# First norm by feature in four units behind raw turned rows

## The reference, cut to what matters

```python
sc, scc = silu(c), silu(c_ctx)                    # one latent, one context condition
for layer in range(2):
    mod_lat = split(sc @ ada_w[layer] + ada_b[layer], 6)     # each (1024,)
    mod_ctx = split(scc @ ada_w[layer] + ada_b[layer], 6)
    h_lat = rms_norm(x, pre_mix_g[layer]) * (1 + mod_lat[1]) + mod_lat[0]
    h_ctx = rms_norm(ctx, pre_mix_g[layer]) * (1 + mod_ctx[1]) + mod_ctx[0]
    p_lat, p_ctx = h_lat @ w_in[layer], h_ctx @ w_in[layer]
    ...   # two attentions per layer, output projection, sandwich norm
    ...   # second modulated norm, convolution feed-forward, norm
```

## Time and profile before

| what | value |
|---|---|
| median of 3 runs | 1719.2 us (1719.05 to 1720.28) |
| the profiled execution | 1719.3 us |
| its span, first to last instruction | 1717.6 us |
| TensorE busy | 1657.2 us, 96% of the span |
| VectorE, ScalarE, GpSimd busy | 1006.1, 637.0, 233.4 us |
| DMA | 211.36 MB, mean 123 GB/s |
| mean granted TensorE clock | 0.992 of full speed |

### The profile page before, as it was taken

The page is one execution under the profiler, slowest core; times in us unless marked ns, Lnnn a source line. Parts: engine busy times, 40 slices in busy tenths (PEclk is TensorE's granted clock), DMA queues, the critical chain, the costliest instruction groups (busy, mean ns, idle before and its releaser), DMA issues.

```text
span 1717.6 us, 26527 instructions
## 1 busy us (share of the span) xinstructions
PE 1657.2 (96%) x9828; PEld 1334.1 (78%) x9828; DVE 1006.1 (59%) x1912; ACT 637.0 (37%) x1123; POOL 233.4 (14%) x378
## 2 busy tenths in 40 slices
PE   6999899999999999999999999998999999999998
PEld 2877566668898888888878878886678888888886
DVE  4655566754747777777776496315753744443445
ACT  3414555653421212121324443225543533333343
POOL 0413233330100000000000023204420100000000
PEclk9999999999999999999999999998999999999999
DMA  8687231266513353434334454323404443332243
GB/s 318 191 275 220 81 91 35 45 89 213 179 50 99 98 147 98 140 105 130 114 101 146 140 183 140 121 88 55 123 16 135 124 122 98 96 95 66 86 135 135
DMA packets 242584, 211.36 MB, mean 123 GB/s; under 512 B 54201, under 2 KB 204601, under 8 KB 242489
## 3 DMA queue, kind: packets, MB, share of 16 engines
q1 hardware_dynamic: 236186, 199.28, 39.0%
q0 software_dynamic: 4288, 9.10, 1.4%
q10 hardware_dynamic: 2016, 1.73, 0.4%
HBM read 186.58 MB, written 23.48 MB: 122 GB/s over the span
## 4 chain that ended last, share of the span: by engine, by line
PE 86%; DVE 5%; ACT 4%; DMA 2%; issue 2%; SPq 1%; POOL 1%; ACTq 0%; DVEq 0%
PE ps L1361 31%; PE ps L889 10%; PE ps L891 10%; PE ps L890 10%; PE ps L1126 4%; PE ps L1237 4%; PE ps L1032 3%; PE ps L1184 3%; PE ps L1371 2%; PE ps L1175 1%; PE ps L1347 1%; PE ps L1346 1%; PE ps L1345 1%; ACT arena L1727 1%; PE ps L946 1%
## 5 line engine op out<-in xcount | busy, mean ns | idle before, releaser
L1903 DVE TENSOR_TENSOR w_lo<-w_raw,w_hi 128x2048 fp32r<-128x2048 f32 (+3 forms) x112 | 204.0, 1822 | 244.0 <-ACT w_hi L1510 243.3
L889 PE MATMUL ps<-w_hi,act_hi 128*128 128x512 f32 (+2 forms) x872 | 337.6, 387 | 2.6 <-DVE act_lo L1903 1.4
L890 PE MATMUL ps<-w_lo,act_hi 128*128 128x512 f32 (+2 forms) x872 | 333.0, 382 | 0.0
L891 PE MATMUL ps<-w_hi,act_lo 128*128 128x512 f32 (+2 forms) x872 | 332.9, 382 | 0.0
L1361 PE MATMUL ps<-act_lo,w_hi 128*128 128x512 f32 (+1 forms) x912 | 277.8, 359 | 0.0
L1361 PE MATMUL ps<-act_hi,w_hi 128*128 128x512 f32 (+1 forms) x912 | 276.2, 357 | 0.0
L1361 PE MATMUL ps<-act_hi,w_lo 128*128 128x512 f32 (+1 forms) x912 | 274.3, 355 | 0.0
L1510 ACT ACTIVATE w_hi<-w_raw 128x2048 fp32r<-128x2048 f32 (+2 forms) x106 | 166.1, 1567 | 270.0 <-PE ps L891 211.9
L889 PEld LDWEIGHTS ps<-w_hi,act_hi 128*128 128x128 f32 x872 | 164.2, 188 | 39.5 <-issue 9.3
L891 PEld LDWEIGHTS ps<-w_hi,act_lo 128*128 128x128 f32 x872 | 164.2, 188 | 30.8
L890 PEld LDWEIGHTS ps<-w_lo,act_hi 128*128 128x128 f32 x872 | 164.4, 189 | 29.3
(11 more groups left out here) (157 smaller groups left out, 2098.4 us busy)
## 6 DMA issues: line engine op xcount, KB each, us to landing
arena<-in_ada_w SPq DMA_DIRECT2D x44, 1024.0 KB, 8.2
w_raw<-in_ffn_up SPq DMA_DIRECT2D x88, 512.0 KB, 5.2
w_raw<-in_ffn_down SPq DMA_DIRECT2D x88, 256.0 KB, 3.0
w_raw<-in_odd_w_in SPq DMA_DIRECT2D x20, 512.0 KB, 4.5
arena<-mods SPq DMA_DIRECT2D x16, 512.0 KB, 7.0
x_after_mix<-arena SPq DMA_DIRECT2D x10, 512.0 KB, 3.0
arena<-x_after_mix SPq DMA_DIRECT2D x10, 512.0 KB, 6.3
wide_raw<-in_ada_w SPq DMA_DIRECT2D x4, 1024.0 KB, 13.8
```

Of the source, the lines that this page charges most:

```text
L889: mm(out_, s_hi, m_hi, start=start, stop=False)
L890: mm(out_, s_hi, m_lo, start=False, stop=False)
L891: return mm(out_, s_lo, m_hi, start=False, stop=stop)
L1903: V.tensor_sub(out_, full, hi.bitcast(fp32)).then_inc(sem_, 1)
```

## The change

The six row tiles are loaded first, each into its own buffer. They are squared, scaled in place by their root alone and turned raw; ScalarE copies the turned rows to `x_turned`. Shift and scale are now applied by feature, as a value per partition. The four modulation units are cut otherwise: unit n holds the 256 columns of shift and the 256 of scale that belong to feature chunks 2n and 2n + 1 (runs of 1 KB instead of 2 KB). `wide_mm(n)` is followed by a copy of its row to SBUF and by `wide_turn(n)`, four small matmuls with a selector that turn the row into columns; VectorE adds the bias and forms (1 + scale) x gain. Then, for each stream, ScalarE writes the high half of chunks 2n and 2n + 1 from the turned rows (two instructions), VectorE computes the full value (two) and subtracts (one), and `products` multiplies these two chunks for all tiles of the stream. `wide_mm(n + 1)` stands ahead of unit n's products. `ada_mm(0)` and `ada_mm(1)` move to the last unit. Identity and selector are asked for right behind the conditions; the first weight unit is asked for behind the rows, the second behind wide unit 2. Five constants are asked for behind unit 1's high halves, five behind unit 2's, one behind unit 3's. Early modulation units 0 and 1 and weight units 2 and 3 now wait for `wide_mm(1)`, early unit 2 for the last low half of the norm. On POOL the root has two instructions instead of one, since the mean and epsilon move there.

```diff
-        wide_row = arena[:, 8 * D:10 * D]
-        wide_raw = [arena[:, 14 * D + n * KC * WIDE:14 * D + (n + 1) * KC * WIDE].rearrange("p (k c) -> p k c", k=KC)
-                    for n in range(2)]
-        wide_raw += [nc.alloc_sbuf_tensor_at(f"wide_raw{n}", [P, KC, WIDE], fp32, offset=act_at + n * 4 * KC * ROWS)
-                     for n in range(2)]
-        sel = sb("sel", [P, 2, P])
+        x_turned = arena[:, 0:KC * ROWS].rearrange("p (k r) -> p k r", k=KC)
+        x_first = [kilo(6 + t) for t in range(NT)]
+        wide_row = arena[:, 22 * D:22 * D + WIDE]
+        wide_raw = [arena[:, n * D:(n + 4) * D].rearrange("p (k c) -> p k c", k=KC) for n in (14, 18, 10, 14)]
+        first_full = nc.alloc_sbuf_tensor_at("first_full", [P, KC, ROWS], fp32, offset=act_at + 4 * KC * ROWS)
+        first_scrap = nc.alloc_sbuf_tensor_at("first_scrap", [P, 2, D], fp32, offset=act_at + 4 * (KC * ROWS + 5 * ROWS))
+        sel = sb("sel", [P, 2])
...
-        ADA_AT = {(1, 5): [0, 1], (2, 1): [2], (2, 3): [3], (2, 5): [4], (3, 1): [5], (3, 3): [6], (3, 5): [7],
+        ADA_AT = {(1, 0): [0], (1, 1): [1], (2, 1): [2], (2, 3): [3], (2, 5): [4], (3, 1): [5], (3, 3): [6], (3, 5): [7],
...
             def wide_unit(n):
-                v = I["ada_w"][0].rearrange("(k p) c -> p k c", p=P)[:, :, n * WIDE:(n + 1) * WIDE]
+                v = I["ada_w"][0].rearrange("(k p) c -> p k c", p=P)
                 for half, (a, b) in enumerate(((0, KC // 2), (KC // 2, KC))):
-                    sp.dma_start(wide_raw[n][:, a:b, :], v[:, a:b, :]).then_inc(wide_in[n][half], 16)
+                    for part in range(2):
+                        src = v[:, a:b, part * D + n * FEATS:part * D + (n + 1) * FEATS]
+                        sp.dma_start(wide_raw[n][:, a:b, part * FEATS:(part + 1) * FEATS], src)\
+                            .then_inc(wide_in[n][half], 16)
+            def first_rows(t):
+                sp.dma_start(x_first[t], x_source("norm0", t)).then_inc(first_in[t], 16)
+            for t in range(NT):
+                first_rows(t)
+            k_unit(0, I["even_w_in"][0], 0, 4, 0, MLA_IN)
             wide_unit(0)
-            sp.wait_ge(wide_clear, 1)
-            sp.dma_start(wide_row[0:2, :], I["ada_b"][0:1, 0:2 * D].to_broadcast([2, 2 * D])).then_inc(wide_bias, 16)
-            for n in range(1, WIDES - 1):
-                wide_unit(n)
-            gain_loads("norm0")
-            wide_unit(WIDES - 1)
-            x_moves("norm0", range(2))
-            for n in range(2):
-                k_unit(n, I["even_w_in"][0], 4 * n, 4, 0, MLA_IN)
-            x_moves("norm0", range(2, NT))
+            wide_unit(1)
+            sp.wait_ge(t_done, 2 * NT)
+            wide_unit(2)
+            k_unit(1, I["even_w_in"][0], 4, 4, 0, MLA_IN)
+            sp.wait_ge(t_done, row_round(0) + 1)
+            wide_unit(3)
...
-            sp.wait_ge(t_free, WIDES)
+            sp.wait_ge(t_done, row_round(1) + 1)
             for i in range(2):
                 early_unit(i)
             for n in (2, 3):
                 k_unit(n, *units[n])
-            sp.wait_ge(h_ready, base("norm0", "h") + NT)
+            sp.wait_ge(first_lo, 2 * WIDES)
...
             def wide_mm(n):
-                ring_free(n)
+                r = row_round(n)
+                ring_free(r)
...
+            def wide_turn(n):
+                r = row_round(n) + 1
+                pe.wait_ge(t_free, r)
+                for c in range(WIDE // P):
+                    last = mm(bank(6 + r % 2, 2, 2 * c), wide_row[:, c * P:(c + 1) * P], sel[:, :], start=True, stop=True)
+                last.then_inc(t_done, 1)
...
-            def first_norm_turns():
+            def first_norm_products():
+                def rows_turn(t):
+                    pe.wait_ge(h_ready, t + 1)
+                    for half in range(2):
+                        r = turn_round(t) + half
+                        turn(r, r, [x_first[t][:, (4 * half + k) * P:(4 * half + k + 1) * P] for k in range(4)])
+                def products(n, tiles, part):
+                    weights(n // 2)
+                    pe.wait_ge(first_lo, part)
+                    for t in tiles:
+                        rows = slice(t * P, (t + 1) * P)
+                        for j in range(FEAT_K):
+                            k, at = n * FEAT_K + j, (n % 2 * FEAT_K + j) * MLA_IN
+                            cols = slice(at, at + MLA_IN)
+                            last = three(bank(t, MLA_IN), act_hi[:, k, rows], act_lo[:, k, rows],
+                                         w_hi[:, n // 2, cols], w_lo[:, n // 2, cols], k == 0, k == KC - 1)
+                        if n % 2:
+                            last.then_inc(mm_done, 1)
+                latent, context = range(LT), range(LT, NT)
                 for t in range(NT):
...
+                    rows_turn(t)
+                wide_mm(0)
+                wide_turn(0)
+                wide_mm(1)
+                products(0, latent, 1)
+                wide_turn(1)
+                products(0, context, 2)
+                wide_mm(2)
+                products(1, latent, 3)
+                wide_turn(2)
+                products(1, context, 4)
+                wide_mm(3)
+                products(2, latent, 5)
+                wide_turn(3)
+                products(2, context, 6)
+                ada_mm(0)
+                products(3, latent, 7)
+                ada_mm(1)
+                products(3, context, 8)
...
+            for dst, src in FIRST:
+                act.dma_start(dst, src, allow_slow_non_contiguous=True).then_inc(ident_in, 16)
...
-            for dst, src in FIRST:
-                act.dma_start(dst, src, allow_slow_non_contiguous=True).then_inc(ident_in, 16)
...
+            def first_norm():
+                def square(t):
+                    act.wait_ge(first_in[t], 16)
+                    at_least(act, sum_x, t - 1)
+                    A(first_scrap[:, t % 2, :], x_first[t], ACT.Square, accum_out=ssx[:, t:t + 1]).then_inc(sum_x, 1)
+                def turned(t):
+                    for half in range(2):
+                        r = turn_round(t) + half
+                        act.wait_ge(t_done, r + 1)
+                        A(x_turned[:, 4 * half:4 * half + 4, t * P:(t + 1) * P],
+                          bank(6 + r % 2).rearrange("p (k r) -> p k r", k=4), ACT.Copy).then_inc(t_free, 1)
+                def hi(n, v):
+                    if v == 0:
+                        act.wait_ge(first_mods, n + 1)
+                    rows = (slice(0, LAT), slice(LAT, ROWS))[v]
+                    for j in range(FEAT_K):
+                        k = n * FEAT_K + j
+                        last = A(act_hi[:, k, rows], x_turned[:, k, rows], ACT.Identity,
+                                 scale=first_mod[:, n, 1, j, v:v + 1], bias=first_mod[:, n, 0, j, v:v + 1])
+                    last.then_inc(first_hi, 1)
+                square(0)
+                square(1)
+                for t in range(NT):
+                    if t + 2 < NT:
+                        square(t + 2)
+                    turned(t)
+                    if t == LT - 1:
+                        w_loaded(0)
+                        split_hi(0, 0, 4 * MLA_IN)
+                for n in range(WIDES):
+                    if n == 2:
+                        w_loaded(1)
+                        split_hi(1, 1, 4 * MLA_IN)
+                    act.wait_ge(t_free, 2 * NT)
+                    for v in range(2):
+                        hi(n, v)
+                    if n:
+                        for dst, src in CONSTS[5 * (n - 1):5 * n]:
+                            act.dma_start(dst, src, allow_slow_non_contiguous=True).then_inc(const_in, 16)
...
             def first_norm():
...
+                def normed(t):
+                    dve.wait_ge(rs_x, t + 1)
+                    V.tensor_scalar(x_first[t], x_first[t], rsx[:, t:t + 1], None, ALU.mult).then_inc(h_ready, 1)
+                def modulation_columns(n):
+                    r = row_round(n)
+                    dve.wait_ge(t_done, r + 1)
+                    V.tensor_copy(wide_row, bank(6 + r % 2, WIDE)).then_inc(t_free, 1)
+                    dve.wait_ge(t_done, r + 2)
+                    m = first_mod[:, n, :, :, :]
+                    V.tensor_add(m.rearrange("p s j v -> p (s j v)"), bank(6 + (r + 1) % 2, 2 * WIDE // P),
+                                 first_bias[:, n, :]).then_inc(t_free, 1)
+                    dve.wait_ge(t_free, r + 2)
+                    V.scalar_tensor_tensor(out=m[:, 1], in0=m[:, 1], scalar=1.0,
+                                           in1=first_gain[:, n].to_broadcast([P, FEAT_K, 2]),
+                                           op0=ALU.add, op1=ALU.mult).then_inc(first_mods, 1)
+                def modulated(n, v):
+                    dve.wait_ge(first_mods, n + 1)
+                    rows = (slice(0, LAT), slice(LAT, ROWS))[v]
+                    for j in range(FEAT_K):
```

(76 more changed lines are left out.)

109 lines of the change are left out of this document (35 added, 74 removed).

## The result

| | before | after |
|---|---|---|
| median, in one session | 1719.74 us (1719.05 to 1720.79, 4 runs) | 1710.37 us (1708.44 to 1711.18, 4 runs) |
| profiled execution, span | 1719.3, 1717.6 us | 1709.8, 1708.2 us |

The ratio is 0.9947 [0.9935, 0.9959], 9.4 us less; 1709.9 was predicted.

What follows compares the result with a forecast made beforehand. TensorE, busy 96% of the span, bounds the kernel except until it is fed without a break. First chain to 29.4, four units 37.1, then finishes put unit 4 at 87.7 instead of 97.1: 1719.3 - 9.4 = 1709.9 us, range 1703.5 to 1716.0.

Steps and rivals of the forecast that it cites:

- Rows first, ScalarE sets the pace: Kernel start: first row block there at 4.9 us, ScalarE sets the pace from about 9, first wide product at 21.
- First unit: From 21 us to the first chunk matmul: 9.9 us at low clock or 6.8 at high; middle taken, 29.4.
- Four units: TensorE from first chunk matmul to second chunk: sum 37.1 us, second chunk at 66.5 instead of 78.1.
- second weight split: Second unit: VectorE's weight split stands ahead of its row copy, ready at 44.4 against 43.9, costing 0.5 us.
- The last constant: Ahead of VectorE's weight split 2: issued at 57.8, landing 4 us later at 61.8, split done at 64.2.
- the term of 0.2: VectorE's weight split behind the last constant is done at 64.2, 0.2 us later than the first finish at 64.0.
- Finishes: VectorE and POOL: two steps of 5.7 us, three of 2.4; unit 2 evacuated at 87.5, unit 4 at 87.7.
- Behind unit 4: After unit 4 only TensorE is in the chain for long, so the 9.4 us gained there reaches the end.
- a late constant: Rival: last constant takes 9.6 us to land, split at 69.8; 3.8 us gained, 1715.5; chance 0.10.
- TensorE alone: Rival: finishes come earlier and hide; 11.6 us gained, 1707.7, or 1706.2 with high clock from 21 us; chance 0.14.
- the low clock in the units: Rival: 36 slow matmuls cost a unit 5.8 us; two units 1721.4, all four plus first chain 1734.4; chance 0.08.
- runs of 1 KB: Rival: 1 KB pieces load at half the rate, wide units 5 us later each; about 1719, no change; chance 0.04.

Runs made afterwards that it cites:

- e6: Changed kernel with wide unit 0 (2.1 MB) asked for ahead of the rows: 1715.14 us, ratio 0.9979.
- e5: Changed kernel with identity and selector asked for behind the exponential, where they were before: 1711.41 us, ratio 0.9957.
- e1: The changed kernel run again with no edit: 1708.55 us, ratio 0.9945.
- e9: e2's kernel with the second half of each turned tile copied by VectorE instead of ScalarE: 1707.65 us, ratio 0.9938.
- e7: Changed kernel with wide product n + 1 and its turn behind all products of unit n: 1728.54 us, ratio 1.0062.
- e2: Changed kernel with POOL's stores of modulation units 0 and 1 one tile later: 1704.52 us, ratio 0.9921.
- e8: Changed kernel with constants in two blocks, five behind unit 1's high halves and six behind unit 3's: 1711.77 us, ratio 0.9953.
- e11: e9's kernel with seven unread 512-column matmuls in TensorE's waits around wide product 0's turn and wide product 1: 1703.53 us, ratio 0.9918.
- e12: e9's kernel with wide unit 0 before first weights, these split later, two latent tiles before wide product 1, nineteen unread matmuls: 1706.56 us.
- e3: Changed kernel with three unread identity matmuls behind each turned row tile: 1710.66 us, ratio 0.9952.

## Why the prediction held, point by point

*Rows first, ScalarE sets the pace:* right, within 0.5 us at each date. e6 and e5 show that what the first chain loses arrives at the second chunk undiminished (6.5 and 3.4 us). e1 and e9 add what the prediction did not see, for it dated the load of wide unit 0 alone: wide unit 1 is close behind that pace (waits of 0.65 and 0.89 us for it), so shortening ScalarE's list alone is soon stopped there.

*First unit:* 29.4 was a middle between two clocks, and after took 29.25 with the low clock in wide product 0 and the high one behind it. That the middle was met so closely is luck: e1, the same kernel, had the high clock throughout and came to 27.70, under the lower bound of 27.9. The sum has a slip as well: its terms add up to 9.7 and 6.8, not 9.9 and 6.8, which gives 30.7, 27.8 and a middle of 29.25.

*Four units:* 37.1 predicted, 37.05 measured. The 0.5 us for the second weight split did not occur: ScalarE's five DMA issues (35.43 to 37.76) ran while it computed high halves (35.33 to 37.8), so the split started at 37.80. That term was wrong, and a wait that the sum took for covered stood in its place: 0.45 us for VectorE's low half ahead of the last unit's products (58.19). There `ada_mm(0)`, 1.07 us, gives less cover than a wide product, 1.92, and ScalarE began its high halves 0.42 us behind the values that they wait for, where in the other units it was 0.1; why, stays open. The two deviations cancel to 0.05 us, which is luck again. e7 prices the cover: 22.8 us.

*The last constant:* it was issued at 55.30 instead of 57.8, since ScalarE's issues run beside its arithmetic, its 4 us to landing were 2.5, VectorE did not wait for it, and the term of 0.2 falls away.

*Finishes:* the mechanism is right (e2: without the two stores in the way the step is 3.1 to 3.2 us and the wait ahead of unit 4 is gone), its step mis-sized: 6.1 us where 5.7 stood. VectorE was through with unit 2 at 88.0 instead of 87.5, and unit 4 came at 88.09, 9.0 us earlier than before where the sum had 9.4.

*Behind unit 4:* "From there I see only TensorE in the chain for long, so what is gained there is gained at the end" failed. The wait itself was in the sum, the clock behind it was not: unit 4 took 0.86 us more and its next matmuls were slow too, 1.4 us in all. That the total came out at 9.4 all the same is luck. After won 0.9 us between the projection's end and layer 1, 1.4 us from the input projection of layer 1 to the last scores, and lost 0.5 us behind them, though the change touches nothing there. The rows put the 1.4 us down to the clock. In both profiles TensorE stands 4.69 us in that stage, and the same sixteen matmuls behind it come out like this, first before, then after:

```profile
1185.54 1.83 PE L1233 MATMUL ps<-arena 128*64 128x128 f32 x16
...
1175.59 1.09 PE L1276 MATMUL ps<-arena 128*64 128x128 f32 x16
```

The windows show a granted clock of 0.50 to 0.73 from 1176 to 1188 us before and of 0.50 to 0.69 from 1166 to 1174 after. Why one execution has the longer stretch stays open; e1, e2, e5 and e6 have it as the kernel before does. By e1's profile the same kernel is 12.6 us ahead of the kernel before (spans 1705.0 and 1717.6), by after's 9.4. So the parts up to unit 4 were foreseen to 0.4 us, and the total was met by deviations that cancel, within a spread of 2.7 us (after, 4 runs) to 4.5 us (e1, 6 runs) between executions of one kernel.

*The rivals:* a late constant is real (e8) and was not met; TensorE alone would have decided with e2's order, 18.99 us between second chunk and unit 4 as in the prediction; the low clock in the units is what e7 shows once the cover is gone, for 52 of the 144 matmuls; runs of 1 KB moved at 347 GB/s, not at half.

## What to carry to other kernels

Load first what starts the longest chain, and put the next block's small products ahead of this block's large ones: here the uncovered edges cost 12 us of waiting and 9 us of low clock. Before work is moved into an earlier stage, look at each engine's list there: two small stores on POOL stood in front of roots and cost 2.8 us until they went one tile back. Where a short wait of TensorE can't be removed, matmuls that nobody reads may pay if they fit into it: in two pairs they went with 1.9 us at the place, and with 4.1 us in one whole time (e11) and 0.1 in the other (e12). Where the clock was high without them they brought nothing (e3). And before one total is read as a forecast come true, the same kernel should be run again: e1 showed which parts of the 9.4 us went with the clock of one execution.

## What the runs showed of the hardware

- After the same wait of 2.73 us in front of unit 4 the granted clock was 0.50 in after and e6 and 1.00 in e1 and e5; behind 2.74 us in e3 and 3.95 us in e8 it was 0.50, and behind 3.49 us in e7 0.50 each time. The Trainium skill, page "TensorE: Matmul & The Clock Gate", section "What's actually happening", says that the slow state is the default and that the number of slow matmuls at a kernel's start varies from run to run for one kernel. These rows, in the middle of a kernel, vary in the same way.
- A load of 1 KB in pieces of 8 bytes, issued at 1.79 us amid the large loads, landed 6.8 us later (6.2 in e1); one of 4 KB, issued at 55.30 when these were nearly done, 2.5 us later (3.5 in e1).
- DMA issues on ScalarE's queue, 0.39 to 0.46 us each, ran beside its own arithmetic: the four high halves of unit 2 took 2.51 us with five issues beside them (after) and without any (e8). Where six issues outlasted the high halves, to 57.42 in e8, the weight split behind them began 0.65 us after these.
